# A three-part transformer kernel: norms taken in at the evacuation, matmuls without use placed in gaps, vector work and attention scores moved, the last down products ordered by token tile

## The reference, cut to what matters

```python
u = attention(rms_norm(h, norm_mix_pre)) ;      h = h + rms_norm(u, norm_mix_post)      # first block
u = relu(rms_norm(h, norm_ffn_pre) @ w_up)**2 @ w_down ; h = h + rms_norm(u, norm_ffn_post)
mods = einsum('bd,lde->lbe', silu(c), ada_w) + ada_b                                    # second block
shift, scale, gate = split(mods[2 * layer], 3)
h = rms_norm_2(x, norm_mix[layer]) * (1 + scale) + shift
y = hgrn2_mixer(h)      # layer 0: q, f, i, g = h @ w_in ; gated recurrence in chunks ; @ w_out
y = nsa_mixer(h, kv)    # layer 1: 16 query and 4 key heads ; compressed + selected + window branch ; @ w_out
x = x + gate * y
shift, scale, gate = split(mods[2 * layer + 1], 3)
x = x + gate * ((silu(a) * b) @ w_out)          # a, b = split(modulate(x) @ w_in), hidden width 2816
```

## Time and profile before

| | us |
|---|---|
| median of 3 runs | 1131.99 |
| the profiled execution, its own time | 1132.07 |
| its span in the trace | 1130.2 |
| TensorE (PE) busy | 1034.1, 91% |
| VectorE (DVE) busy | 782.5, 69% |
| ScalarE (ACT) busy | 503.9, 45% |
| GpSimd (POOL) busy | 111.0, 10% |
| DMA queues | 57.3% of 16 engines, 198 GB/s over the span |

### The profile page before, as it was taken

How to read it: one execution, slowest core, us unless ns; L and a number is a source line. 1 busy time by engine, 2 the same in 40 slices (tenths; PEclk the granted TensorE clock), 3 DMA queues, 4 the chain that set the end, 5 groups by cost and what they waited for, 6 DMA issues and landing times.

```text
span 1130.2 us, 16074 instructions
## 1 busy us (share of the span) xinstructions
PE 1034.1 (91%) x6116; PEld 849.2 (75%) x6116; DVE 782.5 (69%) x1007; ACT 503.9 (45%) x638; POOL 111.0 (10%) x137
## 2 busy tenths in 40 slices
PE   4999979999997999688899999979989898999997
PEld 3887767888885887676678888858867776888886
DVE  6677656787666878887688787887836766554553
ACT  6336335444444575362333344334437734343441
POOL 1000000000001001570200000000930200000000
PEclk9999989999998999899999999989999999999999
DMA  9975228798825976004298888944423133645632
GB/s 315 366 254 193 75 95 334 259 342 290 288 84 214 342 265 229 1 2 168 86 354 280 296 305 288 322 163 149 154 74 115 39 112 111 208 165 187 217 115 74
DMA packets 126670, 224.11 MB, mean 198 GB/s; under 512 B 4792, under 2 KB 58264, under 8 KB 126616
## 3 DMA queue, kind: packets, MB, share of 16 engines
q1 hardware_dynamic: 125960, 221.00, 56.4%
q0 software_dynamic: 656, 2.36, 0.7%
HBM read 222.30 MB, written 1.05 MB: 198 GB/s over the span
## 4 chain that ended last, share of the span: by engine, by line
PE 74%; DVE 14%; POOL 4%; issue 3%; ACT 3%; DMA 0%; SPq 0%; DVEq 0%; ACTq 0%; POOLq 0%
PE psum L1605 71%; DVE adaacc L1083 2%; DVE arena L1123 2%; DVE wlo L1065 2%; ACT whi L703 2%; PE psum L1996 1%; DVE arena L1161 1%; POOL arena L660 1%; POOL arena L569 1%; DVE xlo L1131 1%; PE psum L2154 1%; DVE arena L1343 1%; DVE gain_b L1343 1%; PE psum L1853 1%; DVE res L1171 1%
## 5 line engine op out<-in xcount | busy, mean ns | idle before, releaser
L1065 DVE TENSOR_TENSOR wlo<-raw,whi 128x2048 fp32r<-128x2048 f32 (+1 forms) x170 | 340.4, 2017 | 158.7 <-ACT whi L703 158.4
L1605 PE MATMUL psum<-whi,xhi 128*128 128x512 f32 x880 | 353.3, 401 | 25.9 <-DVE wlo L1065 12.9
L703 ACT CAST whi<-raw 128x2048 fp32r<-128x2048 f32 (+1 forms) x170 | 286.2, 1688 | 181.6 <-PE psum L1605 178.6
L1605 PE MATMUL psum<-whi,xlo 128*128 128x512 f32 x880 | 347.1, 394 | 0.0
L1605 PE MATMUL psum<-wlo,xhi 128*128 128x512 f32 x880 | 347.0, 394 | 0.0
L1605 PEld LDWEIGHTS psum<-whi,xhi 128*128 128x128 f32 x880 | 167.6, 190 | 64.2 <-issue 23.5
L1605 PEld LDWEIGHTS psum<-whi,xlo 128*128 128x128 f32 x880 | 167.8, 191 | 36.3
L1605 PEld LDWEIGHTS psum<-wlo,xhi 128*128 128x128 f32 x880 | 168.1, 191 | 33.2
L1083 DVE SCALAR_TENSOR_TENSOR adaacc<-adaw,cact,adaacc 128x512 f32<-128x512 f32 x196 | 147.3, 752 | 6.8 <-DMA adaw<-in_ada_w 0.2
L1605 PE MATMUL psum<-whi,hhi 128*128 128x512 f32 x304 | 120.0, 395 | 0.0
L1605 PE MATMUL psum<-whi,hlo 128*128 128x512 f32 x304 | 118.4, 389 | 0.0
(11 more groups left out here) (264 smaller groups left out, 979.3 us busy)
## 6 DMA issues: line engine op xcount, KB each, us to landing
adaw<-in_ada_w SPq DMA_DIRECT2D x48, 1024.0 KB, 5.4
raw<-in_ffn_w_in SPq DMA_DIRECT2D x88, 512.0 KB
raw<-in_ffn_w_out SPq DMA_DIRECT2D x44, 512.0 KB
raw<-in_w_up SPq DMA_DIRECT2D x16, 1024.0 KB
raw<-in_w_down SPq DMA_DIRECT2D x16, 1024.0 KB
raw<-in_hgrn_w_in SPq DMA_DIRECT2D x16, 1024.0 KB
raw<-in_attn_w_qkv SPq DMA_DIRECT2D x12, 1024.0 KB
adaw<-in_kv_ada_w SPq DMA_DIRECT2D x8, 1024.0 KB, 5.6
```

The source lines that it names most:

```text
L703: sc.copy(whi[:, s, 0:width], raw[:, s, 0:width]).then_inc(hi_ready[s], 1)
L1065: ve.tensor_tensor(wlo[:, s, 0:width], raw[:, s, 0:width], whi[:, s, 0:width].bitcast(F32), ALU.subtract).then_inc(lo_ready[s], 1)
L1605: return te.matmul(dst, lhsT, rhs, start=start, stop=stop, skip_group_check=open_)
```

## The change

At the start, SP issues only the vector `norm_mix_pre` before the weights, and nine other vector loads go to ScalarE's queue. The first norm and the one ahead of FF1 are deferred: TensorE transposes `res` itself, and `rstd` is applied where the product leaves PSUM (QKV) or in the ReLU's scale (FF1). The transposes for tile 0 of the second of these stand ahead of the last six matmuls of WO. `keep(n, bank)` is new: n matmuls of two constants whose result is never read. It stands ahead of FF1 (20), at HIN's and at the NSA projections' norm (28 and 12). `last_down` is new: the down products of the last round of each MLP are taken by token tile.

```diff
+            def keep(n, bank):
+                for _ in range(n):
+                    mm(psum[:, bank, 0:384], identb[:], causb[:])
             def norm(j, i):
-                pe.wait_ge(n_y, 2 * j + i + 1)
+                if j == 0:
+                    pe.wait_ge(x_in[i], 16)
+                elif j == 1:
+                    pe.wait_ge(p_res, i + 1)
+                else:
+                    pe.wait_ge(n_y, 2 * (j - 2) + i + 1)
+                x = y if j > 1 else res
...
             def project_tiles(n, j, fresh, width=512):
+                keep(28, 6)
                 norm(j, 0)
+                keep(12, 6)
...
+                        if f == 1 and i == 1 and s == 3 and next_norm is not None:
+                            norm(next_norm, 0)
...
             def up_tiles(n, j, fresh, gated=None, gates=0, saved=None):
-                norm(j, 0)
+                if j > 1:
+                    norm(j, 0)
+                if gated is None:
+                    keep(20, 6)
...
+            def last_down(n, kts, h0=0):
+                for i in range(TT):
+                    for s in (2, 3):
+                        item_ready(s, n)
...
             # ScalarE, the start
+            split(0, Q_QKV)
+            norm_high(0, 0)
+            split(1, Q_QKV)
+            norm_high(0, 1)
...
             # ScalarE, FF1
-                    sc.activation(relu[:, i, :], psum[:, (0 if first else 4) + i, :], ACT.Relu).then_inc(act_done, 1)
+                    act.wait_ge(n_rstd, 2 + i + 1)
+                    sc.activation(relu[:, i, :], psum[:, (0 if first else 4) + i, :], ACT.Relu, scale=rstd[:, i:i + 1]).then_inc(act_done, 1)
...
             # VectorE, the start
-            norm_scale(0, 0)
-            norm_scale(0, 1)
-            normed_tile(0, 0, 0, False)
+            affine(0, 0, 0, 0, False)
+            affine(0, 0, 0, 1, False)
+            split(0, Q_QKV)
+            low(0, 0, 0)
+            low(0, 0, 1)
+            split(1, Q_QKV)
             normed_tile(0, 0, 1, False)
...
             # VectorE, HOUT and the border behind it
+            ada(A_HOUT, 0)
+            ada(A_HOUT, 1)
             gate_save(0)
-            ada(A_HOUT, 0)
-            split(1, Q_F2A)
-            ada(A_HOUT, 1)
...
             # VectorE, a SwiGLU MLP's first round
-                if m is not None and first:
-                    ada(m, 1)
...
                 if not last:
                     split(1, t + (q0 + 1), nxt)
+                if m is not None and first:
+                    ada(m, 1)
```

More of the change, by code:

```diff
@@ L1019, in weights @@
                 ins.then_inc(w_e, 1)
+            weights(0)
+            weights(1)
+            act.wait_ge(k_["hid"], 1)
+            act.wait_ge(k_["clear"], 2)
+            for j in range(2):
+                r = slice(64 * j, 64 * j + 60)
+                ins = sc.activation(hidt[r, :], psum[r, 4, 0:CHID], ACT.Silu)
+            ins.then_inc(k_["hidst"], 1)
+            for s in (2, 3):
+                act.nop().then_inc(hi_ready[s], 1)
+                unsent[s] = 1
+            for s in range(4):
+                act.nop().then_inc(hi_ready[s], 1)
             def weights_save(u):
@@ L1496, in _ @@
             gate_save(2, 0)
-            v.wait_ge(k_["hid"], 1)
-            for s in (2, 3):
-                v.nop().then_inc(lo_ready[s], 1)
-            for s in range(4):
-                v.nop().then_inc(lo_ready[s], 1)
             def maxima(u):
@@ L1510, in maxima @@
                 ve.tensor_reduce(m[:, :, 1], psum[:, bank:bank + 2, P:384], AX, ALU.max, negate=True).then_inc(w_m, 1)
+            maxima(0)
+            maxima(1)
+            v.wait_ge(k_["hid"], 1)
+            for s in (2, 3):
+                v.nop().then_inc(lo_ready[s], 1)
+            for s in range(4):
+                v.nop().then_inc(lo_ready[s], 1)
             def scaled(u):
@@ L1694, in part @@
                         ins.then_inc(acc_done, 1)
-                part(0, 0)
-                part(0, 1)
+                if early_high:
+                    pe.wait_ge(hi_ready[0], n + 1)
+                    for low in (False, True):
+                        for i in range(TT):
+                            if low:
+                                item_ready(0, n)
+                            else:
+                                pe.wait_ge(t_x, 4 * turned + 1)
+                            for f in range(2):
+                                for k in range(2):
+                                    o = psum[:, 2 * i + f, :]
+                                    xh, xl = [x[:, k, i * P:(i + 1) * P] for x in (xhi, xlo)]
+                                    wh, wl = [w[:, 0, k * D + f * 512:k * D + f * 512 + 512] for w in (whi, wlo)]
+                                    if low:
+                                        ins = mm(o, xh, wl, False, False)
+                                    else:
+                                        mm(o, xh, wh, k == 0, False)
+                                        mm(o, xl, wh, False, False)
+                    ins.then_inc(used[0], 1)
+                else:
+                    part(0, 0)
+                    part(0, 1)
                 if late is not None:
@@ L1827, in up, with down @@
                         up_part(n, s, i, 4)
-            def down(n, kts, last=False, slots=(2, 3), h0=0):
+            def last_down(n, kts, h0=0):
+                for i in range(TT):
+                    for s in (2, 3):
+                        item_ready(s, n)
+                        for f in range(2):
+                            for k in range(kts):
+                                kt = kts * (s - 2) + k
+                                h = h0 + kt
+                                ins = three(psum[:, 2 * i + f, :], hhi[:, h, i * P:(i + 1) * P], hlo[:, h, i * P:(i + 1) * P],
+                                            s, k * D + f * 512, 512, False, kt == 2 * kts - 1, True)
+                        if i == 1:
+                            ins.then_inc(used[s], 1)
+                        elif s == 3:
+                            ins.then_inc(acc_done, 1)
+            def down(n, kts, slots=(2, 3)):
                 for s in slots:
@@ L1883, in _ @@
             down(Q_FF1 + t - 1, 2, slots=(3,))
-            pe.wait_ge(h_lo, 2 * t + 1)
-            down(Q_FF1 + t, 2, last=True, slots=(2,))
             pe.wait_ge(h_lo, 2 * t + 2)
-            down(Q_FF1 + t, 2, last=True, slots=(3,))
+            last_down(Q_FF1 + t, 2)
             project_tiles(Q_HIN, 2, 2)
```

273 lines of the change are left out of this document (151 added, 122 removed).

## The result

The changed kernel takes 1113.93 us (median of 4 runs, 1111.76 to 1117.38) for 1132.37 of the kernel before (4 runs, 1130.88 to 1133.15): ratio 0.9842, 95% interval [0.9812, 0.9871]. The forecast was 1105, range 1097 to 1116. The profiled execution's own time is 1115.21, 16.9 less than the 1132.07 of before, where the sum said 26.8.

What follows compares the result with a forecast made beforehand. TensorE, busy 1034.1 of 1130.2 us, was taken as the bound, with gains at stage borders. Terms 6.8 + 5.0 + 1.5 + 5.3 + 0.65 + 2.9 + 5.8 − 0.9 − 0.25 = 26.8 off 1132.07 gave 1105, range 1097 to 1116.

Steps and rivals of the forecast that it cites:

- The start: Program start through first matmul: weights issued sooner and first norm deferred bring the first matmul from 20.72 to 13.9; 6.8 us.
- FF1's norm: Border WO to FF1: first matmul 2.2 earlier, 2.4 from 12 matmuls at full clock, 0.4 at transposes; 5.0 us.
- FF1's end: FF1's end and HIN's start: `last_down` stalls cost 2.2, fillers hold the clock; net gain 1.5 us, range 0 to 2.5.
- HOUT and the borders: HOUT and F2A's start: `ada` ahead of gate copy removes wait and slow matmuls, 5.5, less 0.2 for `split(1)`; 5.3 us.
- NSA: NSA stage: keys and scores, pipeline of units, and tail together gain 5.8 us, range 3 to 9.
- keys: NSA's key transposes: 2.84 of waiting and their slow run of 3.48 against 1.9 go; 4.4 us gained.
- the scores ahead: NSA: scores of unit 0, now ahead of the compression, wait for the gate copy; a stall of 1.3 us.
- the loop: NSA's pipeline of units: stalls of some 4.1 become 1.5 as pieces are smaller; 2.6 us gained.
- The tail: NSA from the last compressed output to NOUT's end: 30.0 before, 29.9 after; 0.1 us gained.
- F2B's norm: F2B's norm: `split(1)` ahead of `norm_scale` puts transposes 6.4 behind the residual's start for 5.4; 0.9 us lost.
- clock not held: Rival: clock falls behind the fillers; FF1, HIN and NSA projections lose 8.8 us in all, giving 1114; chance 0.15.
- VectorE gives it back: Rival: moved splits and copies make VectorE last in F2A, F2B and behind the NSA loop; 1110 us; chance 0.14.

Runs made afterwards that it cites:

- ada_later: Changed kernel with TensorE's first `ada` moved behind the first half of QKV's second round; 1110.27 us, ratio 0.9794 to the kernel before.
- constants_later: Changed kernel with ScalarE's second-round casts earlier: slot 0 ahead of squares and constants, slot 1 ahead of constants; 1111.01 us, ratio 0.9799 to the kernel before.
- the second trace of the changed kernel: Trace from running the changed kernel once more, with no edit; 1113.12 us, ratio 0.9828 to the kernel before.
- downs_by_slot: Changed kernel with the last down products of FF1, F2A and F2B by slot again, as in the kernel before; one execution, 1114.40 us.
- more_fillers: `ada_later` without the 20 fillers ahead of FF1, with 12 to 14 fillers in each of three waits of about 2 us; 1104.17 us, ratio 0.9757.

## Why the prediction held in its range and missed in its size

The range held the time, near its upper end; the forecast of 1105 was 9 us below the median and 10 below the profiled execution, which the pieces below add up to. Of these 10, 9 are one step.

*The start* is the step that failed. "No later stall" was in it without a word: the 6.8 were kept whole since "the stage behind is TensorE's". I had followed the splits of the next round, and left out `ada`, which stands on VectorE between them and on TensorE right behind the first round. The first matmul came 1 us later than forecast, because slot 0 was full at 9.96 and not at 8.9; cast, split and the first `low` then took what I had given them:

```profile
9.96 1.90 ACT L697 CAST whi<-raw 128x2048 fp32r<-128x2048 f32 x1 [3.74 <-DMA raw<-in_attn_w_qkv]
```

And 8.0 were lost in QKV: 4.44 waiting, 2.8 at the low clock behind it, 0.3 by two more slow matmuls in the first round, and the rest in `ada`'s own matmuls at the low clock. `ada_later` and `constants_later` give 7.2 and 7.1 back at QKV's end (5.9 and 5.8 against the second trace of the changed kernel), and 3 to 5 us of the median.

*FF1's norm* came out at 5.2 for 5.0; the fillers there cost 1.0 and bring nothing, so the 2.4 for the clock were right and were put down to the wrong edit. The twelve slow matmuls before stood behind a gap of 4.23, which the early transposes with the deferred norm shorten to 1.10 without a filler. That a larger gain and an unforeseen loss add up to nearly the forecast is luck.

*FF1's end*: `last_down`'s loss was priced 2.2 and measured 1.9, the fillers' gain 2.6. What made this piece +0.4 are nine slow matmuls at 180, 1.8 us; the second trace has none there and gives −1.2. In the recurrence (+1.3) the waits are the same in both kernels, but TensorE is busy 48.7 us at a mean clock of 0.87 for 47.4 at 0.89; `downs_by_slot` has 47.3 at 0.92 there. The sum had no term for clock behind gaps that stay.

*HOUT and the borders*: 5.6 for 5.3. The copy's order carries 3.5; the split behind the residual brings 1.0 where I charged 0.2, and at NOUT 0.5 where I charged part of 0.9. I had priced what it does to GpSimd and not what it frees: the residual. On GpSimd its step took 0.98 for 0.19, from 908.73 to the end of VectorE's split at 909.7. The Trainium skill's rule of the shared port pair ("SBUF — State Buffer", "Who interferes with whom") says so for a VectorE instruction with two inputs in SBUF; the trace agrees.

*NSA*: keys 4.6 for 4.4; the scores ahead cost 1.0 for 1.3; the loop won 4.4 for 2.6, so ScalarE at 2.7 to 2.8 a unit did not hold it up. That its smaller pieces are what won the 4.4, and that `kt2`'s own place is what won the 4.6, was argued from the waits and not tested by a run. The tail lost 0.5 instead of winning 0.1, and F2B's norm came out as charged.

*The rivals*: the clock behind the fillers was held, 1.00 at HIN from 353.30 and no slow matmul at the projections; the rival "clock not held" failed there, but low clock came back in QKV and FF1, behind gaps without fillers. The Trainium skill ("TensorE: Matmul & The Clock Gate", Part 1) says the number of cold matmuls varies from run to run; the traces agree, with 6 to 14 slow at the start and nine or none behind one wait. Of its other half, small value, the runs show 4.5 us (0.4%) for all fillers as placed, of which the traces place 2.3, and 3.2 for the new ones in `more_fillers`. The rival that VectorE gives it back came true in part: the new wait of 2.47 in F2A (0.85 off the sum), and behind the NSA loop waits of 1.63 for `xlo` and 2.07 for `wlo` in NOUT where one of 1.90 for GpSimd stood before; the loop itself kept its gain. The signs named were otherwise as said: no wait for `adaacc` in HOUT, transposes at HIN 1.09 long, fillers 0.17 apart, and a wait of 1.32 for `gain_b`.

Open: what the waits of 2.21 and 2.47 for `adaacc` in FF1 and F2A would bring if removed and not filled, what `kt2`'s place and the loop's new order bring one by one, and why a wait of about 2 us is followed by slow matmuls in some traces only; none of this was tried.

## What to carry to other kernels

When a stage starts earlier, list everything that TensorE waits for up to the stage's end, side work included, and follow each of it back on its own engine: an engine that was hidden by the late start is the first to show. Before a filler, shorten the gap; put fillers only in waits that nothing else fills, ahead of the instruction that waits and not behind it. When work is moved behind something, price what it frees as well as what it blocks.

## What the hardware showed that I had not expected

Behind a gap of 2.21 us TensorE ran at 1.2 GHz in one execution (nine matmuls 0.43 apart, clock 0.54 over the stretch) and at 2.4 GHz in another of the same kernel (1.00), and in the kernel before. I had counted on slow matmuls only behind gaps of about 4 us and more. From 40 to 44 us the DMA engines ran at 381 GB/s with a share of 1.02, and still were not what QKV waited for: `ada_later` ends it 7.2 sooner.

```profile
40.00:44.00 4.00, 0.18 (x6) 0.21 (x7) 3.89 (x6) 1.98 (x2) 0.00 (x0) 0.99 1.02 381
```
